# Feed-forward stages: the second down chunk is rounded in quarters ahead of the last tiles' work

## The chip, the cores and the metric

One NeuronCore of a Trainium2 chip runs one program. The metric is the device time of one execution in microseconds; the median of three runs of the kernel before is 2256.84 us (2256.57 to 2262.26). All arithmetic is on float32 data. Engines are called PE (matmul), PEld (PE's weight load), DVE, ACT, POOL and SP (it issues DMAs).

## The reference, cut to what matters

The reference is a chain of two blocks over 256 latent tokens (and 256 context tokens in the first) of width 1024. The first has a latent attention and a short convolution layer, each with a mixture of 32 experts; the second has a state-space mixer, a feed-forward layer, a dilated attention and a second feed-forward layer. The change touches the two feed-forward layers of the second block:

```
u = causal_depthwise_conv(h @ w_up, conv_w)      # 1024 -> 2 x 2816, 3 taps
gate, val = u[..., :2816], u[..., 2816:]
y = (silu(gate) * val) @ w_down                  # 2816 -> 1024
x = x + y
```

A root-mean-square norm stands ahead of it, and another, of the sum, behind it.

## The kernel before, in words

**Three products.** A float32 product runs on PE as three products in the format fp32r. Each operand is split in a high half (a rounded copy) and a low half (what the rounding left): high x high, high x low, low x high, summed in one bank (`product3`, line 574 and on; its matmul is line 584). The high half of a weight chunk is made by ACT (`round_scalar`, its instruction is line 297), the low half by DVE as a subtraction (`rest_vector`, line 303). The same work exists in quarters: `round_piece_scalar` (line 312) and `rest_piece_vector` (line 320) do the columns of piece q of four, and piece 3 marks the whole as ready. `product3` waits for the high half of the weights ahead of its first and second products and for the low half ahead of the third.

**The ring.** Weights arrive by DMAs that SP issues (line 274) into a ring of 6 slots of 128x4096 floats. A chunk takes two slots: the raw data, later overwritten by the low half, and the high half. So three chunks are there at a time, and the fetch of a chunk waits until PE has finished the chunk three before it.

**The feed-forward stage** (class `Ffn`). `w_up` has 11 chunks, each for two tiles of 128 channels of gate and value (22 tiles, m = 0 to 21). `w_down` has 6 chunks: number 0 has 2 of the 22 row tiles of H (128x2048 a slot), numbers 1 to 5 have 4 each (128x4096), in the order 0 and 1, 2 to 5, ..., 18 to 21. PE does the up tiles one after the other, 48 matmuls each, then the down chunks in order; within a chunk it goes over the 8 tiles of the result, each with its own bank, which stays open over all chunks. So the 8 result banks are all taken, and the first down matmul waits until the bank of the last up tile has been copied. Chunk 0 is 48 matmuls, the others 96.

Per up tile m, ACT copies the bank into `PB` (line 2747), DVE does six instructions of taps (lines 2776 and 2779) into `acc`, ACT does the silu (line 2726), POOL multiplies (line 2801) to `H`, ACT makes its high half (line 2728) and POOL its low half (line 2803).

**The order on the engines** is written out by hand. Each engine runs its list in order, and each instruction waits on counters of the others. On ACT, step m of the loop is: on even m the rounding of the next chunk (m = 20 rounds down chunk 0), `make_h(m - 2)` (silu and high half), then the copy of tile m. Behind the loop come `make_h(20)`, `make_h(21)`, the roundings of down chunks 1 to 5, and the first rounding of the next stage (`then.prepare_scalar`). On DVE, step m is: on even m the remainder of that chunk, then the taps of tile m once ACT has copied it; behind the loop the remainders of down chunks 1 to 5 and of the next stage's first chunk, then the eight additions to the residual (line 2788). POOL has the two operations of each tile, in order.

Of the kernel before, what the change touches and what calls it, by code (L numbers as in the profile page):

```python
# [62 lines left out]
KFF = FFN // P  # L63
# [670 lines left out]
class Start:  # L734
# [8 lines left out]
    def scalar(self, e, w):  # L743
        k, a = self.k, self.k.a
        e.dma_start(k.cols[:, :], a["cols"]).then_inc(*k.constants.up())
        e.dma_start(k.mats[:, :, :], a["mats"]).then_inc(*k.constants.up())
        e.dma_start(k.rows[:, :], a["rows"].broadcast_to([P, a["rows"].shape[1]])).then_inc(*k.constants.up("constants"))
        w.wait_ge(*k.constants.at("constants"))
        w.wait_ge(*k.pool.at("cond zero"))
        e.activation(k.silu_cond[:, :, 0:2], k.col("cond"), ACT.Silu).then_inc(*k.act.up("silu cond"))  # L750
# [5 lines left out]
    def vector(self, e, w):  # L756
        w.wait_ge(*self.k.constants.at("constants"))
# [459 lines left out]
class Moe:  # L1217
# [590 lines left out]
    def more_scalar(self, e):  # L1808
        if isinstance(e, Count):
            return  # L1810
        scalar, cap, (rows, turned, x_turned, _) = self.more["scalar"].sem, self.cap, self.more_banks()
        with e.If(self.more_flag(e) > 0):
            self.more_begin(e)
            for n in range(self.n_blocks - 1):
                with e.Fori(0, EXPERTS, 1) as x:
                    it = x + n * EXPERTS
                    e.wait_ge(*self.more_count("matmul", it, 2))
                    e.activation(self.h[0][0:cap, :], rows[cap:2 * cap, :], ACT.Silu).then_inc(scalar, 1)
                    e.wait_ge(*self.more_count("matmul", it, 3))
                    e.activation(k_flat(self.ht[0]), turned[:, 0:KF * cap], ACT.Copy).then_inc(scalar, 1)  # L1820
                    e.wait_ge(*self.more_count("matmul", it, 4))
                    e.activation(self.y[0], x_turned[:, :], ACT.Copy).then_inc(scalar, 1)
                    e.wait_ge(*self.more_count("vector", it, 6))
            for m in range(KD):
                self.squares.square(e, m, self.k.X[:, m, 0:self.T]).then_inc(scalar, 1)
            e.wait_ge(*self.more_count("matmul", (self.n_blocks - 1) * EXPERTS, 1))

    def more_vector(self, e):
        if isinstance(e, Count):
            return  # L1830
        vector, cap, (rows, turned, x_turned, _) = self.more["vector"].sem, self.cap, self.more_banks()
        with e.If(self.more_flag(e) > 0):
            self.more_begin(e)
# [804 lines left out]
class Ffn:  # L2638
# [78 lines left out]
    def scalar(self, e, w):  # L2717
        k, T, key = self.k, SEQ, self.key
        pe, act, dve, pool, banks = k.pe, k.act, k.dve, k.pool, k.banks
        k.meet(w, self.before)  # L2720
        k.norm_parts_scalar(e, w, key, lambda i: k.A[:, i, 0:T], self.x_parts[0])

        def make_h(m):
            s = m % 4
            w.wait_ge(*dve.at(key, "taps", m))
            e.activation(self.acc[:, s, 0, :], self.acc[:, s, 0, :], ACT.Silu).then_inc(*act.up(key, "silu", m))
            w.wait_ge(*pool.at(key, "h", m))
            e.activation(self.H_high[:, m, :].bitcast(F32R), self.H[:, m, :], ACT.Copy).then_inc(*act.up(key, "h high", m))  # L2728

        w.wait_ge(*pool.at(key, "pads"))  # L2730
        for m in range(KFF):
            s = m % 4
            if m % 2 == 0:
                (self.w_up + self.w_down)[m // 2 + 1].round_scalar(e, w)
            if m >= 2:
                make_h(m - 2)
            if m >= 4:
                w.wait_ge(*dve.at(key, "taps", m - 4))
            if m < 2:
                for j in range(2):  # L2740
                    w.wait_ge(*pe.at(key, "up", m, j))
                    e.activation(self.PB[:, s, j, self.pad:], banks.of(key, "up", m, j)[:, 0:T], ACT.Copy
                                 ).then_inc(*act.up(key, "up", m, j))
                act.mark(key, "up", m)
            else:
                w.wait_ge(*pe.at(key, "up", m))
                e.activation(self.PB[:, s, :, self.pad:], banks.of(key, "up", m)[:, :].rearrange("p (j t) -> p j t", j=2),
                             ACT.Copy).then_inc(*act.up(key, "up", m))
        make_h(KFF - 2)
        make_h(KFF - 1)  # L2750
        for chunk in self.w_down[1:]:
            chunk.round_scalar(e, w)
        if self.then:
            self.then.prepare_scalar(e, w)
        for m in range(KD):
            self.squares.square_scalar(e, w, m, k.X[:, m, 0:T], dve.at(key, "out", m))
        k.root_scalar(e, w, ("ffn out", self.layer), T)
        act.mark("end", key)

    def vector(self, e, w):  # L2760
        k, T, key = self.k, SEQ, self.key
        pe, act, dve, pool, banks = k.pe, k.act, k.dve, k.pool, k.banks
        k.meet(w, self.before)
        w.wait_ge(*dve.now())
        k.norm_parts_vector(e, w, key, lambda i: k.A[:, i, 0:T], k.col("ffn_norm")[:, self.layer, :], *self.x_parts)
        taps = k.col("ffn_conv_w")
        for m in range(KFF):
            s = m % 4
            if m % 2 == 0:
                (self.w_up + self.w_down)[m // 2 + 1].rest_vector(e, w)  # L2770
            if m >= 4:
                w.wait_ge(*pool.at(key, "h", m - 4))
            w.wait_ge(*act.at(key, "up", m))
            for j in range(2):
                buf, w3 = self.acc[:, s, j, :], taps[:, self.layer, j * KFF + m, :]
                e.tensor_scalar(buf, self.PB[:, s, j, 0:T], w3[:, 0:1], None, ALU.mult).then_inc(*dve.up())
                for q in (1, 2):
                    w.wait_ge(*dve.now())
                    e.scalar_tensor_tensor(buf, self.PB[:, s, j, q:q + T], w3[:, q:q + 1], buf, ALU.mult, ALU.add  # L2779
                                           ).then_inc(*dve.up())  # L2780
            dve.mark(key, "taps", m)
        for chunk in self.w_down[1:]:
            chunk.rest_vector(e, w)
        if self.then:
            self.then.prepare_vector(e, w)
        for m in range(KD):
            w.wait_ge(*pe.at(key, "out", m))
            e.tensor_tensor(k.X[:, m, 0:T], banks.of(key, "out", m)[:, 0:T], k.X[:, m, 0:T], ALU.add
                            ).then_inc(*dve.up(key, "out", m))
        k.root_vector(e, w, ("ffn out", self.layer), T)  # L2790
        dve.mark("end", key)
# [580 lines left out]
```

## Time and profile before

| | |
|---|---|
| median of the runs | 2256.84 us (2256.57 to 2262.26) |
| the profiled execution | 2263.14 us, its span 2261.3 us |
| busy: PE, DVE, ACT, POOL | 94%, 44%, 32%, 11% of the span |
| mean granted clock of PE | 0.97 |
| matmuls, all of PE | 13462 |

Times of the rows below are counted from the start of the span of the profiled execution. A view can be asked for a stretch of the span. The first feed-forward stage's down chunks lie near 1775 to 1850 us, the second's near 2178 to 2250 us. A granted clock of 1.00 is 2.4 GHz, 0.50 is 1.2 GHz.

### The profile page before, as it was taken

What the parts mean: (1) busy time and instruction counts of PE and PEld (TensorE: products, weight loads), DVE (VectorE), ACT (ScalarE), POOL (GpSimd) and SP (SyncE); (2) the same over time, 40 slices, a digit from 0 to 9 for tenths busy, and PEclk for the clock granted to TensorE, in tenths of its full rate; (3) what the DMA queues carried; (4) which work ended last, traced back from release to release, by engine and by line L of the source; (5) the groups of instructions that cost most, each with busy time, mean ns of one, the idle gap of its engine ahead of it and who ended that gap; (6) DMA issues with size and microseconds to landing.
All of it is one profiled execution on the core that took longest, in us unless ns stands there. A gap on an engine that the chain in (4) does not pass through costs nothing. (4 is left out here: it accounts for less than half of the span.)

```text
span 2261.3 us, 31171 instructions
## 1 busy us (share of the span) xinstructions
PE 2118.1 (94%) x13462; PEld 1487.5 (66%) x13462; DVE 1003.7 (44%) x1647; ACT 717.6 (32%) x1073; POOL 244.4 (11%) x220
## 2 busy tenths in 40 slices
PE   5999999999998898999999988988899889999988
PEld 3745644444443795444444438966899889998987
DVE  3434411111110654111111118866589656777983
ACT  3234211111111542111111128855455444445542
POOL 0000000000000000000000000065136200003630
PEclk9999899999999998999999999999999989999999
DMA  9777699999999567999999984421445444334542
GB/s 326 258 271 261 246 415 421 421 421 421 421 421 383 187 223 297 418 421 421 421 420 421 421 340 166 161 97 53 149 150 187 168 170 127 98 128 158 184 147 94
DMA packets 216208, 616.86 MB, mean 273 GB/s; under 512 B 20224, under 2 KB 107392, under 8 KB 166656
## 3 DMA queue, kind: packets, MB, share of 16 engines
q1 hardware_dynamic: 208960, 612.01, 70.3%
q10 hardware_dynamic: 7104, 2.76, 0.4%
q8 instruction: 110, 1.80, 0.3%
q14 instruction: 34, 0.28, 0.0%
HBM read 613.69 MB, written 1.05 MB: 272 GB/s over the span
## 5 line engine op out<-in xcount | busy, mean ns | idle before, releaser
L1328 PE MATMUL bank<-ring,arena 128*64 128x512 f32 x2048 | 454.4, 593 | 12.2 <-DMA ring<-in_moe_w_up 12.0
L584 PE MATMUL bank<-normed_rounded,ring_rounded 128*128 128x256 f32 x3424 | 416.5, 283 | 4.9 <-ACT normed_rounded L680 3.4
L584 PEld LDWEIGHTS bank<-normed_rounded,ring_rounded 128*128 128x128 f32 x3424 | 412.1, 189 | 6.9 <-issue 4.3
L303 DVE TENSOR_TENSOR ring_rounded<-ring,ring_rounded 128x4096 fp32r<-128x4096 f32 (+2 forms) x68 | 295.3, 4347 | 131.5 <-ACT ring_rounded L297 131.3
L1328 PEld LDWEIGHTS bank<-ring,arena 128*64 128x64 f32 x2048 | 149.4, 137 | 305.6 <-issue 304.7
L1674 DVE TENSOR_TENSOR arena<-arena,bank 64x512 f32<-64x512 f32 x64 | 43.6, 681 | 660.9 <-ACT arena L1498 660.9
L584 PE MATMUL bank<-arena_rounded,ring_rounded 128*128 128x256 f32 x2336 | 296.5, 287 | 19.2 <-DVE ring_rounded L303 6.9
L584 PEld LDWEIGHTS bank<-arena_rounded,ring_rounded 128*128 128x128 f32 x2336 | 288.1, 193 | 22.4 <-DVE ring_rounded L303 7.5
L297 ACT ACTIVATE ring_rounded<-ring 128x4096 fp32r<-128x4096 f32 (+2 forms) x68 | 234.7, 3455 | 58.0 <-DMA ring<-in_ffn_w_down 51.3
L1337 PE MATMUL bank<-ring,arena 128*64 128x512 f32 x1024 | 235.6, 602 | 3.8 <-ACT arena L1505 3.8
L1498 ACT ACTIVATE arena<-bank 64x512 f32<-64x512 f32 x64 | 38.1, 595 | 449.1 <-PE bank L1328 449.1
L1337 PEld LDWEIGHTS bank<-ring,arena 128*64 128x64 f32 x1024 | 68.2, 137 | 123.8 <-issue 110.9
L572 PEld LDWEIGHTS bank<-mats,arena 128*128 128x128 f32 (+2 forms) x662 | 84.6, 166 | 79.2 <-issue 66.3
L1352 PE MATMUL bank<-arena 64*128 64x256 f32 x1024 | 127.8, 388 | 1.4 <-ACT arena L1512 1.4
L1512 ACT ACTIVATE arena<-bank 128x512 f32<-128x512 f32 x64 | 38.3, 598 | 276.8 <-PE bank L1337 276.8
L572 PE MATMUL bank<-mats,arena 128*128 128x128 f32 (+2 forms) x662 | 103.0, 278 | 8.7 <-POOL arena L2414 5.4
L1352 PEld LDWEIGHTS bank<-arena 64*128 64x128 f32 x1024 | 93.2, 186 | 23.8 <-issue 11.7
L2779 DVE SCALAR_TENSOR_TENSOR arena<-arena,cols 128x256 f32<-128x256 f32 x176 | 95.3, 541 | 6.3
L2803 POOL TENSOR_TENSOR arena_rounded<-arena,arena_rounded 128x256 fp32r<-128x256 f32 x44 | 92.8, 2110 | 23.3 <-ACT arena_rounded L2728 23.3
L1307 PE MATMUL bank<-arena_rounded 128*128 128x256 f32 x512 | 78.3, 298 | 0.0
L1307 PEld LDWEIGHTS bank<-arena_rounded 128*128 128x128 f32 x512 | 65.5, 190 | 5.0 <-issue 1.2
L1505 ACT ACTIVATE arena<-bank 128x256 f32<-128x256 f32 x64 | 24.7, 386 | 132.5 <-PE bank L572 132.5
(274 smaller groups left out, 2082.7 us busy)
## 6 DMA issues: line engine op xcount, KB each, us to landing
ring<-in_moe_w_gate SPq DMA_DIRECT2D x128, 1024.0 KB, 16.7
ring<-in_moe_w_up SPq DMA_DIRECT2D x128, 1024.0 KB, 19.0
ring<-in_moe_w_down SPq DMA_DIRECT2D x128, 1024.0 KB, 18.3
ring<-in_w_mod SPq DMA_DIRECT2D x24, 2048.0 KB, 11.5
ring<-in_ffn_w_up SPq DMA_DIRECT2D x44, 1024.0 KB, 7.5
ring<-in_ssm_w_in SPq DMA_DIRECT2D x12, 2048.0 KB, 8.1
ring<-in_ffn_w_down SPq DMA_DIRECT2D x10, 2048.0 KB, 7.8
ring<-in_conv_w_in SPq DMA_DIRECT2D x6, 2048.0 KB, 9.0
```

The lines of the kernel that those rows point to most:

```text
L297: e.activation(ring.rounded[(self.number + 1) % RING][:, 0:n].bitcast(F32R), ring.slots[self.number % RING][:, 0:n], ACT.Copy).then_inc(*s ...
L303: e.tensor_tensor(ring.rounded[slot][:, 0:n].bitcast(F32R), ring.slots[slot][:, 0:n], ring.rounded[(self.number + 1) % RING][:, 0:n], ALU. ...
L572: return e.transpose(out, in_, self.mats[0:rows, 0, 0:rows])
L584: end = e.matmul(out, lhs.bitcast(F32R), rhs.bitcast(F32R), start=start and n == 0 and k == 0, stop=stop and n == 2 and k == n_k - 1)
L1307: end = e.matmul(out, f[:, t, feats].bitcast(F32R), mine[:, t, hot].bitcast(F32R), start=t == 0 and f is self.f_high, stop=t == self.NT - ...
L1328: ends[i] = e.matmul(bank[rows, :], xt[:, n * KD // 2 + j, :], weights[:, j, :], start=n == 0 and j == 0, stop=n == 1 and j == KD // 2 - 1)
L1337: end = e.matmul(bank[n * cap:(n + 1) * cap, :], self.ht[x][:, k, :], weights[:, i, n * 512:(n + 1) * 512], start=k == 0, stop=k == KF - 1)
L1352: end = e.matmul(self.acc(kk), self.y[x][rows, i * P:(i + 1) * P], self.back[x][rows, :], start=False, stop=last and kk % 2 == 1)
L1512: e.activation(self.y[x % 2], banks.of(key, "y", x)[:, :], ACT.Copy).then_inc(*act.up(key, "y", x))
L1674: e.tensor_tensor(h, h, banks.of(key, "h", x)[0:cap, :], ALU.mult).then_inc(*dve.up(key, "h", x))
L2779: e.scalar_tensor_tensor(buf, self.PB[:, s, j, q:q + T], w3[:, q:q + 1], buf, ALU.mult, ALU.add).then_inc(*dve.up())
L2803: e.tensor_tensor(self.H_low[:, m, :].bitcast(F32R), self.H[:, m, :], self.H_high[:, m, :], ALU.subtract).then_inc(*pool.up(key, "h low", m))
```

## The change

In both feed-forward stages the rounding of down chunk 1 is cut in four pieces and moved forward. On ACT, piece 0 goes between the high half of tile 19 and the copy of tile 21, pieces 1 to 3 between that copy and `make_h(20)`. On DVE, the four remainders go between the wait for the copy of tile 21 and the taps of tile 21. The loops behind go over chunks 2 to 5. PE, POOL and SP keep their lists.

```diff
@@ scalar @@
             if m >= 2:
                 make_h(m - 2)
+            if m == KFF - 1:
+                self.w_down[1].round_piece_scalar(e, w, 0)
             if m >= 4:
                 w.wait_ge(*dve.at(key, "taps", m - 4))
...
+        for q in (1, 2, 3):
+            self.w_down[1].round_piece_scalar(e, w, q)
         make_h(KFF - 2)
         make_h(KFF - 1)
-        for chunk in self.w_down[1:]:
+        for chunk in self.w_down[2:]:
             chunk.round_scalar(e, w)
@@ vector @@
             w.wait_ge(*act.at(key, "up", m))
+            if m == KFF - 1:
+                for q in range(4):
+                    self.w_down[1].rest_piece_vector(e, w, q)
             for j in range(2):
...
-        for chunk in self.w_down[1:]:
+        for chunk in self.w_down[2:]:
             chunk.rest_vector(e, w)
```

## Rows read from the trace of the kernel before

**Rows 1.** The page, part 4: shares of the span by engine and line.

```profile
PE bank L584 22%; DVE ring_rounded L303 2%; ACT ring_rounded L297 1%; PE bank L2136 1%; PE bank L2944 1%; PE bank L618 1%; DVE arena L2484 1%; PE bank L619 1%; PE bank L2968 1%; DVE ring_rounded L320 1%; PE bank L2887 1%; PE bank L624 1%; PE bank L572 0%; PE bank L2987 0%; PE bank L2208 0%; PE bank L2158 0%
```

**Rows 2.** Timeline of PE: start us, us, engine, line, operation, count, [idle before, releaser].

```profile
1775.53 5.91 PE L584 MATMUL bank<-arena_rounded,ring_rounded 128*128 128x256 f32 x48 [0.78 <-ACT arena L2747]
1784.40 1.21 PE L584 MATMUL bank<-arena_rounded,ring_rounded 128*128 128x256 f32 x8 [2.97 <-ACT ring_rounded L297]
1788.86 49.15 PE L584 MATMUL bank<-arena_rounded,ring_rounded 128*128 128x256 f32 x400 [3.25 <-DVE ring_rounded L303]
1840.08 10.31 PE L584 MATMUL bank<-arena_rounded,ring_rounded 128*128 128x256 f32 x72 [2.07 <-DVE residual L2788]
...
2191.71 57.63 PE L584 MATMUL bank<-arena_rounded,ring_rounded 128*128 128x256 f32 x472 [3.21 <-DVE ring_rounded L303]
```

**Rows 3.** The chain of waits, 1755 to 1860: start us, us, what.

```profile
1780.84 3.52 ACT ring_rounded L297
...
1823.84 7.74 DMA ring<-in_w_kv
```

**Rows 4.** Timeline of SP, the fetches of down chunks 1, 3, 4, 5; then 3, 4-5.

```profile
1763.39 0.37 SPq L274 DMA_DIRECT2D ring<-in_ffn_w_down  x1
...
1781.47 0.37 SPq L274 DMA_DIRECT2D ring<-in_ffn_w_down  x1
1801.12 0.37 SPq L274 DMA_DIRECT2D ring<-in_ffn_w_down  x1
1812.48 0.37 SPq L274 DMA_DIRECT2D ring<-in_ffn_w_down  x1
...
2184.33 0.37 SPq L274 DMA_DIRECT2D ring<-in_ffn_w_down  x1
2203.94 11.73 SPq L274 DMA_DIRECT2D ring<-in_ffn_w_down  x2
```

**Rows 5.** Windows: stretch us, PE, PEld, DVE, ACT, POOL busy (count), PEclk, DMA, GB/s.

```profile
1788.86:1790.00 1.14, 1.14 (x5) 1.14 (x6) 1.14 (x1) 1.07 (x1) 0.00 (x0) 0.50 0.00 0
...
1812.50:1823.80 11.30, 11.30 (x98) 11.30 (x97) 4.42 (x1) 2.59 (x1) 0.00 (x0) 1.00 0.50 187
...
1840.10:1843.00 2.90, 2.90 (x13) 2.90 (x14) 0.26 (x1) 0.71 (x2) 0.73 (x1) 0.50 0.74 277
```

**Rows 6.** Timeline of ACT at the end of the up tiles.

```profile
1772.31 0.42 ACT L2728 ACTIVATE arena_rounded<-arena 128x256 fp32r<-128x256 f32 x1 [2.32 <-POOL arena L2801]
1774.79 0.60 ACT L2747 ACTIVATE arena<-bank 128x512 f32<-128x512 f32 x1 [2.06 <-PE bank L584]
...
1780.75 7.11 ACT L297 ACTIVATE ring_rounded<-ring 128x4096 fp32r<-128x4096 f32 x2
```

**Rows 7.** Lines 312 and 320 over the whole span: ns min/median/max.

```profile
L312 ACT ACTIVATE ring_rounded<-ring x28: 1038/1046/1072, 41.2 to 1587.1; 128x1024 fp32r<-128x1024 f32 x28
L320 DVE TENSOR_TENSOR ring_rounded<-ring,ring_rounded x28: 1212/1225/2196, 42.3 to 1589.9; 128x1024 fp32r<-128x1024 f32 x28
```

**Rows 8.** Landings: the tile in_ffn_w_down over the span, and the page's part 6.

```profile
DMA to landing us min/median/max: 4.7/7.8/9.0
...
ring<-in_moe_w_up SPq DMA_DIRECT2D x128, 1024.0 KB, 19.0
```

**Rows 9.** Timeline of DVE.

```profile
1757.10 4.97 DVE L303 TENSOR_TENSOR ring_rounded<-ring,ring_rounded 128x4096 fp32r<-128x4096 f32 x1
...
1775.49 0.35 DVE L2776 TENSOR_SCALAR arena<-arena,cols 128x256 f32<-128x256 f32 x1 [0.36 <-ACT arena L2747]
...
1778.10 1.00 DVE L2779 SCALAR_TENSOR_TENSOR arena<-arena,cols 128x256 f32<-128x256 f32 x2
1784.38 13.10 DVE L303 TENSOR_TENSOR ring_rounded<-ring,ring_rounded 128x4096 fp32r<-128x4096 f32 x3 [5.28 <-ACT ring_rounded L297]
```

**Rows 10.** Timeline of POOL.

```profile
1758.32 4.35 POOL L2803 TENSOR_TENSOR arena_rounded<-arena,arena_rounded 128x256 fp32r<-128x256 f32 x1 [0.53 <-ACT arena_rounded L2728]
...
1777.05 0.87 POOL L2803 TENSOR_TENSOR arena_rounded<-arena,arena_rounded 128x256 fp32r<-128x256 f32 x1 [0.53 <-ACT arena_rounded L2728]
```

## The prediction

> **What bounds the kernel now.** I read the page first: its chain that ended last gives line 584, the three-product matmul on PE, 22% of the span, by far the largest line [rows 1]. So time is won only where PE stands idle or runs slowly. The second view is PE's timeline at the end of the first feed-forward stage [rows 2]. There PE does the 48 matmuls of down chunk 0 until 1775.53 + 5.91 = 1781.44, waits 2.97 us for ACT, does 8 matmuls, and waits 3.25 us for DVE; the second stage shows the same (3.21 us before its 472 matmuls). After that comes one long run. The third view, the chain of waits over the same stretch [rows 3], says what ended those waits: ACT's rounding of down chunk 1, then DVE's remainder of it, and nothing else between 1780.84 and 1788.86. It also shows a later link that the change leaves alone: the fetch of the next stage's first chunk, its rounding, and the wait that it causes.
>
> The fourth view is SP's timeline [rows 4]: a down fetch is issued when PE has finished a chunk, so the issues clock the chunks. The fetch at 1781.47 marks the end of chunk 0, that at 1801.12 the end of chunk 1, that at 1812.48 the end of chunk 2. Chunk 1 therefore took 19.65 us, and chunk 2, of the same 96 matmuls, 11.36 us. In the second stage it is 2203.94 - 2184.33 = 19.61 us against (11.73 - 0.37) = 11.36 us. The difference, 8.29 and 8.25 us, is more than the two waits (2.97 + 3.25 = 6.22). The fifth view, the windows with the granted clock [rows 5], shows where the other 2 us are: after the second wait PE is granted 0.50 (1.2 GHz), against 1.00 (2.4 GHz) in chunk 2. The 88 matmuls from 1788.86 to 1801.12 took 12.26 us, where 88/96 of 11.36 is 10.41.
>
> **The change part by part.** Each of the two stages gets the same edits, so I work out the first one.
>
> *Piece 0 on ACT, in front of the copy of up tile 21.* ACT has finished the high half of tile 19 at 1772.31 + 0.42 = 1772.73 and then stood idle 2.06 us until PE released the copy at 1774.79 [rows 6]. A piece of 128x1024 costs 1.046 us on ACT [rows 7]. Chunk 1 was asked for at 1763.39 [rows 4]; a down chunk landed 4.7 to 9.0 us after its issue, median 7.8 [rows 8], so by 1772.4 at the latest. Piece 0 runs 1772.7 to 1773.7, inside the idle time: cost nothing. Without that cover (a late landing) everything behind it waits: the copy, the last taps, and PE, since chunk 0 started only when that copy had emptied its bank. That is a rival below. SP's issues stay where they are, because what they wait for (PE's up tiles and chunk 0) does not move.
>
> *Pieces 1 to 3 on ACT.* Behind the copy, which ends at 1775.39, come 3 x 1.046, each starting some 0.1 before the last ends as ACT's pairs do: 1775.3 to 1778.2. The high half of chunk 1 is complete at 1778.2, 3.2 us before PE asks for it at 1781.44. What is queued behind the pieces is the silu and high half of tile 20, 2.9 us later; only POOL's product of tile 20 and the last down chunk (tiles 18 to 21) wait for that, and PE reached the last chunk near 1835. Cost nothing.
>
> *Four pieces on DVE, in front of the taps of tile 21.* DVE's row is 1.225 us each [rows 7]; in a run of three remainders 13.10 us passed, not 3 x 4.42 = 13.26, so each starts 0.08 early: 4 x 1.225 - 4 x 0.08 = 4.58 us. They start at 1775.49, where the taps started [rows 9], and the low half is complete at 1780.1, 1.4 us before PE finishes chunk 0. Both waits of PE are gone, and with them the idle time ahead of the slow clock. Chunk 1 takes what chunk 2 took: gain 8.29 us.
>
> *What is late next.* The taps of tile 21 took from 1775.49 to 1778.10 + 1.00 = 1779.10, 3.61 us, and now start at 1780.07, so end at 1783.68. From their end to the start of the next rounding on ACT (silu, POOL's product, high half) it was 1780.75 - 1779.10 = 1.65 us [rows 6, 9]. That rounding is now chunk 2's: it starts at 1785.33 and, at half of the 7.11 us that two such take, ends at 1788.9. DVE's remainder, 4.42, ends at 1793.35. PE finishes chunk 1 at 1781.44 + 11.36 = 1792.80, and asks for the low half after 8 of 96 matmuls, at 1793.75. The slack is 0.40 us. Below, the cost can't be under nothing, since PE can't start chunk 2 before chunk 1 is done. Above, POOL's operations can add to it. Before, two of POOL's (one is the 0.87 us of [rows 10]) ran inside those 3.61 us; if one more gets in the way, the remainder is 0.87 late and PE stands 0.47 us. I take 0.1, near the zero end, and keep 0.5 for each stage. Such a wait costs itself only: the 0.78 us wait before chunk 0 was followed by 48 matmuls in 5.91 us.
>
> Chunk 3 is not touched: its fetch at 1781.47 stays, it is rounded on ACT until 1792.6 and its remainder ends at 1793.4 + 4.4 = 1797.8, while PE wants it at 1804.2. Chunks 4 and 5 are fetched when chunks 1 and 2 end, so they move with PE and keep their distance: chunk 4 is issued at 1792.8, and with 9.0 + 3.6 + 4.4 is ready at 1809.8 against 1815.5. The next stage's first chunk (the 7.74 us fetch of [rows 3], its rounding, and the 2.07 us wait of PE with the clock of 0.50 behind it, [rows 2, 5]) hangs on the end of chunk 3 and moves whole. So the gain passes to the next stage undiminished, and the second stage ends in PE work alone.
>
> *The rule of the Trainium skill weighed.* POOL's remainder of a tile at 1758.32 took 4.35 us and ended 0.6 us after DVE's remainder of a chunk (1757.10 + 4.97), where the one at 1777.05, beside the taps, took 0.87 [rows 9, 10]. The Trainium skill ("SBUF — State Buffer", section "SBUF: two separate sides") says that GpSimd and a DVE operation with two SBUF inputs take a shared pair of ports in turn, one blocking the other for its whole instruction. By that rule, which the row bears out, POOL's product of tile 20 stands still while DVE's pieces run, or slips between two of them and delays the rest. The first costs nothing here; the second is the 0.47 us above.
>
> **Sum.** Gain 8.29 + 8.25 = 16.54, less 2 x 0.1: 16.3 us. The profiled execution took 2263.14 us (span 2261.3 and 1.8 around it); it becomes 2246.8. The median of the runs shown is 2256.84, 6.3 us under the profiled one, whose time is close to the highest run, 2262.26. Nothing in these terms depends on that difference, so I take them off the median: 2240.5 us.
>
> **Rivals.**
> - *The clock is not given back.* The waits go, 2 x 6.2 = 12.4 us, but the granted clock falls somewhere else in the now unbroken run: 2244.4. For it: PE's load rises. Against: chunks 2 and 3 ran at 1.00 in an equally dense run. 7%.
> - *Chunk 2's remainder takes the place of chunk 1's.* If the DVE and POOL collisions come to more than I think, PE stands before chunk 2. A wait like the 2.07 us one brought the clock down to 0.50, and the 72 matmuls behind it took 10.31 us instead of 72/96 x 11.36 = 8.5. Some 2.1 + 1.8 = 3.9 us per stage then come off: 16.5 - 7.8 = 8.7 gained, 2248.1. For it: the slack is 0.40 us. Against: it needs 2.5 us of slip, three of POOL's operations. 8%.
> - *Slower: piece 0 waits for its data.* It stands on ACT before the copy that frees PE's last bank. From 1774.79 - 1.05 - 1763.39 = 10.35 us to landing on, each further microsecond delays chunk 0 by as much. It ends above today's time from some 17 us on: with the 19.0 us that the expert chunks took [rows 8], chunk 0 starts 8.65 us late and, after such idle time, 1.8 us slow; chunk 1 ends at 1781.44 + 8.65 + 1.8 + 11.36 = 1803.25, 2.1 us later than today, 4.3 us over both stages: 2261.1. Against: those landings belong to a stretch with many fetches at once, and no down chunk took over 9.0 us. 2%.
> - *The change does nothing that counts*, as the gain is taken back by a transfer in the attention stage: 2256.8. Against: every fetch of the ring is issued on PE's progress and moves with it. 3%.
>
> **How the numbers follow.** The forecast gets 80%. From no wait at all (2240.3) over 0.5 us in each stage (2241.3) it spans little by itself; the runs of before differ by 5.7 us, and a median may sit at either side. I take 2237.5 to 2248.5, which holds the first two rivals. A measurement of this kernel tells about 0.3%, 6.8 us, from no change. Faster by more: the forecast, the clock rival, and the chunk 2 rival (8.7 us), 95%, of which I take 1 off to the middle for its edge: 94%. Within: 4%. Slower: 2%.
>
> **What would show it.** In the profile after, no wait of PE for the rounding or remainder of down chunk 1 in either stage; down issues some 11.4 us apart from the fourth to the sixth; granted clock 1.00 from chunk 0 to chunk 4; ACT's copy of up tile 21 released by PE, not by piece 0; DVE's last taps ending 4.6 us later behind chunk 0's start; the remainder of chunk 2 ending within 0.5 us of PE's need. I am wrong if piece 0 is released by a DMA after the copy was due, if PE waits over 1 us before chunk 2, or if the span shrinks by under 12 us.

## The result, and the profile after

The changed kernel took 2244.76 us in the median of five runs (2242.49 to 2247.20), against 2256.84 (2256.32 to 2262.26) of the kernel before. The ratio on record is 0.9931, with a 95% interval of 0.9918 to 0.9945; the two medians alone give 0.9946, just outside it. Five runs more of it, beside fourteen of the kernel before, gave 0.9918 (0.9906 to 0.9931). The gain is under 1%, but both intervals leave out 1. The forecast, 2240.5 of 2256.84, is 0.9928 and lies in both intervals; its range held the time.

The profiled execution took 2242.49 us. Its PE timeline answers [rows 2]. The first stage's block of 456 matmuls (54.23 us) now runs without a wait up to the last chunk, of which 24 matmuls are done by then, and the second stage has no wait at all (528 matmuls).

```profile
1772.94 54.23 PE L584 MATMUL bank<-arena_rounded,ring_rounded 128*128 128x256 f32 x456 [0.78 <-ACT arena L2749]
1829.28 10.30 PE L584 MATMUL bank<-arena_rounded,ring_rounded 128*128 128x256 f32 x72 [2.11 <-DVE residual L2795]
...
2165.90 62.77 PE L584 MATMUL bank<-arena_rounded,ring_rounded 128*128 128x256 f32 x528 [0.78 <-ACT arena L2749]
```

SP's timeline, as in [rows 4]: the fetches of chunks 3 and 4, then 5, of the first stage. Chunk 1 lasts from 1778.89 to 1778.89 + (11.73 - 0.37) = 1790.25, 11.36 us where it was 19.65, and chunk 2 ends at 1801.65, 11.40 later.

```profile
1778.89 11.73 SPq L274 DMA_DIRECT2D ring<-in_ffn_w_down  x2
1801.65 0.37 SPq L274 DMA_DIRECT2D ring<-in_ffn_w_down  x1
```

The windows of the first stage, columns as in [rows 5], over chunk 1, the first matmuls of chunk 2, and the rest of it. The granted clock is 1.00 throughout.

```profile
1778.80:1790.10 11.30, 11.30 (x98) 11.30 (x97) 5.88 (x7) 7.47 (x4) 1.49 (x2) 1.00 0.54 196
1790.10:1791.20 1.10, 1.10 (x12) 1.10 (x11) 1.10 (x2) 0.52 (x1) 0.00 (x0) 1.00 0.00 0
1791.20:1801.60 10.40, 10.40 (x90) 10.40 (x90) 4.19 (x2) 3.63 (x1) 0.00 (x0) 1.00 0.54 202
```

The timelines of ACT and then of DVE show the moved pieces (lines 312 and 320) and what is queued behind them. They answer [rows 6] and [rows 9].

```profile
1770.05 1.04 ACT L312 ACTIVATE ring_rounded<-ring 128x1024 fp32r<-128x1024 f32 x1
1772.20 0.60 ACT L2749 ACTIVATE arena<-bank 128x512 f32<-128x512 f32 x1 [1.11 <-PE bank L584]
1772.70 2.95 ACT L312 ACTIVATE ring_rounded<-ring 128x1024 fp32r<-128x1024 f32 x3
...
1782.82 3.61 ACT L297 ACTIVATE ring_rounded<-ring 128x4096 fp32r<-128x4096 f32 x1
```

```profile
1772.90 5.18 DVE L320 TENSOR_TENSOR ring_rounded<-ring,ring_rounded 128x1024 fp32r<-128x1024 f32 x4 [0.35 <-ACT arena L2749]
1778.01 0.83 DVE L2783 TENSOR_SCALAR arena<-arena,cols 128x256 f32<-128x256 f32 x1
...
1780.18 1.01 DVE L2786 SCALAR_TENSOR_TENSOR arena<-arena,cols 128x256 f32<-128x256 f32 x2
1786.46 8.76 DVE L303 TENSOR_TENSOR ring_rounded<-ring,ring_rounded 128x4096 fp32r<-128x4096 f32 x2 [5.28 <-ACT ring_rounded L297]
```

POOL's product of tile 20 asked for the same time as DVE's third and fourth piece:

```profile
1776.03 0.98 POOL L2808 TENSOR_TENSOR arena<-arena 128x256 f32<-128x256 f32 x1 [5.06 <-ACT arena L2726]
```

Piece 0 ran inside idle time and left 1.11 us of it; PE still releases the copy. The low half of chunk 2 was ready at 1786.46 + 4.42 = 1790.88 (17.94 us after the first down matmul). Counted from SP's fetch, as the prediction does it, PE wanted it at 1790.25 + 0.95 = 1791.20, 0.3 us later. That overstates the slack: the experiment with all four of ACT's pieces behind the copy puts it under 0.1 us.

**Where the 20.65 us between the two profiled executions went.** I cut each span at four marks: PE's first down matmul of either stage (before: 1775.53 and 2178.39; after: 1772.94 and 2165.90) and the first matmul of the norm behind it (1850.76 and 2249.71; 1839.94 and 2229.01). The first stage's stretch went from 75.23 to 67.00, 8.2 us less, the second's from 71.32 to 63.11, 8.2 less. The other 4.3 us lie in unchanged code: 2.6 before the first mark (where piece 0 is the only thing changed) and 1.7 in the attention stage.

### The profile page after: what moved, and what is told of

Read it like the earlier page. It is cut to its first block and busy times, and to the rows that moved or that the text cites. A ratio compares the mean times of both kernels' runs of the same rounds, so it can differ in the third digit from the quotient of the medians.

```text
span 2240.7 us, 31183 instructions
## 1 busy us (share of the span) xinstructions
PE 2109.5 (94%) x13462; PEld 1481.8 (66%) x13462; DVE 1003.7 (45%) x1653; ACT 718.4 (32%) x1079; POOL 244.7 (11%) x220
## 5 line engine op out<-in xcount | busy, mean ns | idle before, releaser
L303 DVE TENSOR_TENSOR ring_rounded<-ring,ring_rounded 128x4096 fp32r<-128x4096 f32 (+2 forms) x66 | 286.6, 4345 | 115.2 <-ACT ring_rounded L297 115.0
L584 PE MATMUL bank<-arena_rounded,ring_rounded 128*128 128x256 f32 x2336 | 290.9, 284 | 6.8 <-ACT arena_rounded L1927 2.6
L584 PEld LDWEIGHTS bank<-arena_rounded,ring_rounded 128*128 128x128 f32 x2336 | 283.3, 190 | 9.2 <-ACT arena_rounded L1927 3.4
L297 ACT ACTIVATE ring_rounded<-ring 128x4096 fp32r<-128x4096 f32 (+2 forms) x66 | 227.7, 3450 | 39.4 <-DMA ring<-in_ffn_w_down 32.8
```

Source lines behind the costliest of these rows:

```text
L297: e.activation(ring.rounded[(self.number + 1) % RING][:, 0:n].bitcast(F32R), ring.slots[self.number % RING][:, 0:n], ACT.Copy).then_inc(*s ...
L303: e.tensor_tensor(ring.rounded[slot][:, 0:n].bitcast(F32R), ring.slots[slot][:, 0:n], ring.rounded[(self.number + 1) % RING][:, 0:n], ALU. ...
L584: end = e.matmul(out, lhs.bitcast(F32R), rhs.bitcast(F32R), start=start and n == 0 and k == 0, stop=stop and n == 2 and k == n_k - 1)
```

## The experiments

All of them are read by the same marks. "Stage" is the stretch from the first down matmul to the norm's matmul of the second stage, 71.3 us before and 63.1 after.

**The changed kernel again.** No edit. 

> The changed kernel once more. Theory (the whole change is the two waits and the slow clock of down chunk 1, 8.2 us in each feed-forward stage, and the rest of what single runs show is scatter of stages that the change does not touch): PE's down matmuls again run as one block of 456 in the first stage and 528 in the second, with 62.77 us for the 528 as in the first profile of it; from PE's first down matmul to the final norm's matmul 63.1 us in the second stage against 71.3 before. Median near 2244, where the middle of nine or ten runs of each kernel differs by 12 to 17 us. Rival (something of the gain is given back in a stage behind): the stretch from the first stage's end to the second's begin is longer by 2 to 4 us than the 338.3 us of before.

Measured: a median of 2241.36 us against 2261.05, ratio 0.9918. The stages took 67.14 and 63.11, the attention stretch 325.86, against 327.63 before and 325.96 in the first profile of the change. (The 338.3 of the expectation was counted from another mark, PE's last chunk of the first stage; there it is 338.31 before and 336.51 here.) Nothing was given back behind the first stage: the rival falls.

**One stage at a time.** The edits of the change under `if self.layer == 0`, or 1:

```diff
-            if m == KFF - 1:
+            if m == KFF - 1 and self.layer == 0:
                 self.w_down[1].round_piece_scalar(e, w, 0)
...
-        for chunk in self.w_down[2:]:
+        for chunk in self.w_down[2 if self.layer == 0 else 1:]:
```

> The change in the first feed-forward stage alone. Theory: the first stage is 8.2 us shorter and all behind it as before; the second stage keeps its waits of 3.0 and 3.2 us and 19.6 us for down chunk 1. Time: half of the whole change's gain, 6 to 8 us under before. Rival (the gain is given back in the attention stage behind it): under 4 us.

> The change in the second feed-forward stage alone. Nothing but the final norm stands behind it, so nothing can give the gain back: 8.2 us under before in the stage. Theory: its gain and that of the other stage alone are equal and add to that of the whole. Rival: this one gains 8, the other less.

The first stage alone: ratio 0.9960 (0.9946 to 0.9974), stretches of 67.34 and 71.09. The second alone: 0.9966 (0.9953 to 0.9979), 75.25 and 63.10. Each is worth about the half, and 0.40% + 0.34% = 0.74% stands beside the 0.82% of the whole change, timed next to the same runs of before. In the trace of the first, the untouched stage keeps both waits. Its 8 matmuls between them took 1.66 us instead of the 1.21 of [rows 2], at a granted clock of 0.50 from 2175.50 to 2176.50, so the clock had already fallen before the second wait:

```profile
2174.93 1.66 PE L584 MATMUL bank<-arena_rounded,ring_rounded 128*128 128x256 f32 x8 [2.96 <-ACT ring_rounded L297]
2179.39 57.41 PE L584 MATMUL bank<-arena_rounded,ring_rounded 128*128 128x256 f32 x472 [2.80 <-DVE ring_rounded L303]
```

**DVE's remainders behind the last taps.** This keeps ACT's part of the change and takes DVE's back.

```diff
@@ vector @@
-            if m == KFF - 1:
-                for q in range(4):
-                    self.w_down[1].rest_piece_vector(e, w, q)
...
+        for q in range(4):
+            self.w_down[1].rest_piece_vector(e, w, q)
         for chunk in self.w_down[2:]:
```

> ACT's four pieces stay moved forward; DVE's four remainders of down chunk 1 go back behind the taps of tile 21, in front of chunk 2's remainder. Theory, in times from the first down matmul: the taps end at 3.6, the remainders at 3.6 + 4.6 = 8.2, and PE wants the low half at 5.7 + 0.95 + 0.2 = 6.9: a wait of 1.3 us at the ninth matmul of chunk 1, too short to bring the granted clock down, nothing before chunk 2. 6.9 us gained in each stage, 2.6 us less than the whole change. Rival (any idle time of PE here brings the clock down): 2 us more lost in each stage, that is 6.6 less than the whole change.

Ratio 0.9945 (0.9932 to 0.9959), stage 66.88, 3.8 us more than with the whole change. The wait was 2.03 us where I had said 1.3, as DVE's four remainders took 6.26 us and not 4.6, and the clock fell, as the rival had it:

```profile
1776.19 6.26 DVE L320 TENSOR_TENSOR ring_rounded<-ring,ring_rounded 128x1024 fp32r<-128x1024 f32 x4
```

PE's timeline and its windows behind the wait:

```profile
1773.61 6.86 PE L584 MATMUL bank<-arena_rounded,ring_rounded 128*128 128x256 f32 x56 [0.78 <-ACT arena L2749]
1782.51 49.12 PE L584 MATMUL bank<-arena_rounded,ring_rounded 128*128 128x256 f32 x400 [2.03 <-DVE ring_rounded L320]
```

```profile
1782.50:1784.00 1.50, 1.50 (x11) 1.50 (x12) 0.00 (x0) 1.50 (x1) 0.55 (x1) 0.86 1.01 407
1784.00:1785.00 1.00, 1.00 (x6) 1.00 (x6) 0.00 (x0) 1.00 (x1) 0.00 (x0) 0.50 1.02 406
```

So ACT's part is worth 4.4 of the 8.2 us, and DVE's part the other 3.8: the wait, 0.2 for the break in the block, and 1.5 of clock (in the second stage the 472 matmuls took 57.64 us, where 62.77 less 56 matmuls' 6.6 is 56.1).

**All four of ACT's pieces behind the copy.**

```diff
@@ scalar @@
-            if m == KFF - 1:
-                self.w_down[1].round_piece_scalar(e, w, 0)
...
-        for q in (1, 2, 3):
+        for q in range(4):
```

> All four of ACT's pieces behind the copy of up tile 21, none ahead of it. Times from the first down matmul, going by the trace of the changed kernel (chunk 1 ends at 17.3, chunk 2's low half is ready at 17.9 and wanted at 18.2, slack 0.3): DVE's first piece starts 0.85 us later, so the low half of chunk 1 is ready at 6.3 against 6.9 (no wait), and that of chunk 2 at 18.8: PE waits 0.5 us before the low product of chunk 2, the granted clock stays at 1.00. The second stage takes 0.5 us more than the 63.1 of the changed kernel. Rival (piece 0 ahead of the copy is worth its full 1.05 us, or nothing): 1.0 or 0.0 us more.

Ratio 0.9928 (0.9911 to 0.9944); stage 64.09, 1.0 us more. The wait is where the theory has it, ahead of the low products of chunk 2, but 0.74 instead of 0.5:

```profile
1771.48 18.23 PE L584 MATMUL bank<-arena_rounded,ring_rounded 128*128 128x256 f32 x152 [0.78 <-ACT arena L2747]
1790.44 36.24 PE L584 MATMUL bank<-arena_rounded,ring_rounded 128*128 128x256 f32 x304 [0.74 <-DVE ring_rounded L303]
```

DVE's first piece came 0.97 us later than in the changed kernel (0.93 after the first down matmul, against 0.04 before it), not 0.85, and the second stage grew by 0.98 us, all of it. So piece 0's place is worth its full 1 us, as the rival had it, and the slack before chunk 2 was next to nothing instead of 0.3 us. Two rows show where the 0.3 came from: the matmuls of these blocks in the changed kernel (ns min/median/max), and DVE's remainders of chunks 2 and 3 in this one.

```profile
L584 PE MATMUL bank<-arena_rounded,ring_rounded x87: 277/280/285, 1779.8 to 1789.9; 128*128 128x256 f32 x87
```

```profile
1785.96 8.76 DVE L303 TENSOR_TENSOR ring_rounded<-ring,ring_rounded 128x4096 fp32r<-128x4096 f32 x2 [5.28 <-ACT ring_rounded L297]
```

A matmul is shown 0.28 us long, but the next one starts 0.12 us behind its start (96 in 11.36 us). SP's fetch comes when the last matmul of a chunk has ended, and by then PE has been in the next chunk for some 0.2 us. Without a wait the 153rd matmul would have started 18.23 - 0.28 + 0.12 = 18.07 us after the first. It starts 0.06 us after DVE's remainder has ended here (1790.44 against 1785.96 + 4.42), and in the changed kernel that remainder ended at 17.94: a slack of under 0.1 us. For the same reason a break in a block costs some 0.2 us beside the wait that the row shows.

**Chunk 1 whole.**

```diff
@@ scalar @@
+        self.w_down[1].round_scalar(e, w)      # in place of the four pieces, behind the copy
         make_h(KFF - 2)
@@ vector @@
             if m == KFF - 1:
-                for q in range(4):
-                    self.w_down[1].rest_piece_vector(e, w, q)
+                self.w_down[1].rest_vector(e, w)
```

> Down chunk 1 rounded whole at the same places: ACT behind the copy of tile 21, DVE in front of the taps. Theory (quarters matter because DVE can start a quarter into ACT's work, and each engine's list has little slack): the low half is ready at 7.8 to 8.4 after the first down matmul against 6.9 wanted, a wait of 0.9 to 1.5; the taps end later, chunk 2's low half is ready near 21.4 and wanted at 19.5, a wait of 2.0, which brings the granted clock down for another 1.8 us: second stage 5.0 us longer than the changed kernel's 63.1. Rival (splitting buys nothing, moving forward is all): 0 to 1 us longer.

Ratio 0.9944 (0.9927 to 0.9961), stage 66.24, 3.1 us more than the changed kernel, against a forecast of 5.0. There were two waits, 1.12 and 1.53, and the clock did not fall: the theory's places were right, the second wait 0.5 shorter, its 1.8 us of clock wrong. This kernel also has nothing ahead of the copy; beside the kernel with all four pieces behind it (64.09) the whole chunk costs 2.1 us, and that is what the quarters save.

```profile
1781.95 11.62 PE L584 MATMUL bank<-arena_rounded,ring_rounded 128*128 128x256 f32 x96 [1.12 <-DVE ring_rounded L303]
1795.11 36.23 PE L584 MATMUL bank<-arena_rounded,ring_rounded 128*128 128x256 f32 x304 [1.53 <-DVE ring_rounded L303]
```

**DVE slipped, by 8 and by 16 instructions.**

```diff
                 e.tensor_scalar(buf, self.PB[:, s, j, 0:T], w3[:, 0:1], None, ALU.mult).then_inc(*dve.up())
+                for _ in range(8 if m == KFF - 1 and j == 0 else 0):
+                    w.wait_ge(*dve.now())
+                    e.tensor_scalar(buf, self.PB[:, s, j, 0:T], w3[:, 0:1], None, ALU.mult).then_inc(*dve.up())
```

> The changed kernel with one instruction of the taps of tile 21 (0.35 us, the same values again) repeated eight times on DVE. Theory (slack of 0.3 us before chunk 2, and a wait of 2 us or more costs 1.8 us of slow clock beside itself): the low half of chunk 2 is 3.0 to 3.6 us later, PE waits 2.7 to 3.3 us there and runs at a granted clock of 0.50 behind it, 4.5 to 5.1 us per stage. Rival (the granted clock falls only where the waits come in pairs, as before): 2.7 to 3.3 us per stage.

> As b_slip, with 16 repeated instructions instead of 8. b_slip's wait of 2.89 us before the low products of chunk 2 left the granted clock at 1.00, while 2.03 us after the eighth matmul of chunk 1 was followed by 0.50. Theory (length counts once it is long enough, as the 4.05 us of c_late_fetch was): a wait of 6.0 us, a granted clock of 0.50 behind it, and the 304 matmuls take 37.6 to 38.2 us instead of 36.23. Rival (the place decides, after a long unbroken run a wait costs only itself): 36.2 us.

With 8, the extra row is 3.08 us long, the wait 2.89 and the stage 66.21, 3.1 more: the whole slip, with no slack to take off. The ratio is 0.9966 (0.9953 to 0.9978). Behind that wait of 2.89 us the granted clock is 1.00 in every window, and the 304 matmuls take their 36.23 us. The rival's price held. Its reason, that only paired waits bring the clock down, did not: a single wait of 2.03 us did so in the kernel with DVE's remainders behind the taps. The extra row, then PE:

```profile
1780.36 3.08 DVE L2786 TENSOR_SCALAR arena<-arena,cols 128x256 f32<-128x256 f32 x8
```

```profile
1795.54 36.23 PE L584 MATMUL bank<-arena_rounded,ring_rounded 128*128 128x256 f32 x304 [2.89 <-DVE ring_rounded L303]
...
2191.67 44.76 PE L584 MATMUL bank<-arena_rounded,ring_rounded 128*128 128x256 f32 x376 [2.89 <-DVE ring_rounded L303]
```

With 16, PE waited twice, 2.49 for ACT's half of chunk 2 and 3.25 for DVE's, as it did before the change for chunk 1; I had overlooked ACT. The clock fell to 0.50 and the 304 matmuls took 38.38 us, 2.2 more than at full clock; in the second stage the 376 took 47.46, 2.7 more than the 44.76 above. The stage was 72.02, and the only run, 2262.11 us, is close to the kernel before (2261.58): the slip has put the old pair of waits one chunk later.

```profile
1794.83 1.21 PE L584 MATMUL bank<-arena_rounded,ring_rounded 128*128 128x256 f32 x8 [2.49 <-ACT ring_rounded L297]
1799.29 38.38 PE L584 MATMUL bank<-arena_rounded,ring_rounded 128*128 128x256 f32 x304 [3.25 <-DVE ring_rounded L303]
1839.91 8.78 PE L584 MATMUL bank<-arena_rounded,ring_rounded 128*128 128x256 f32 x72 [2.24 <-DVE residual L2798]
```

In its second stage the clock fell behind the first wait alone, 2.48 us after 17.27 us of matmuls: the 8 matmuls behind it took 1.86 us, and the granted clock in them was 0.50.

```profile
2196.39 1.86 PE L584 MATMUL bank<-arena_rounded,ring_rounded 128*128 128x256 f32 x8 [2.48 <-ACT ring_rounded L297]
2200.85 47.46 PE L584 MATMUL bank<-arena_rounded,ring_rounded 128*128 128x256 f32 x376 [2.60 <-DVE ring_rounded L303]
```

```profile
2196.80:2198.20 1.40, 1.40 (x7) 1.15 (x6) 1.40 (x1) 1.40 (x1) 0.00 (x0) 0.50 1.00 401
```

**The fetch of chunk 1 late**, with piece 0 ahead of the copy and, in a second kernel, with all four behind it as above.

```diff
         for chunk in self.w_up + self.w_down:
+            if chunk is self.w_down[1]:
+                w.wait_ge(*self.k.pe.at(self.key, "up", KFF - 2))
             chunk.fetch(e, w)
```

> The changed kernel, but SP issues the fetch of down chunk 1 when PE has finished up tile 20 instead of 19, 5.7 us later. This tries the rival on the other side: piece 0 stands ahead of the copy and waits for its data. Theory: with 7.8 us to landing the data is there 2.1 us after the copy was due, piece 0 ends 3.1 us after it, the copy and the first down matmul are 3.1 us late, and after 3.9 us of idle time the granted clock falls: 3.1 + 1.8 = 4.9 us per stage against the changed kernel, some 10 in all; still some 6 us under before. Rival (the landing takes under 5.7 us, as the 4.7 of a small chunk): nothing.

> As c_late_fetch, but with all four of ACT's pieces behind the copy of up tile 21. Theory (what makes a late landing dear is that piece 0 stands ahead of the copy): the first down matmul is on time with a wait of 0.78 us instead of 4.05; DVE's pieces end 7.0 to 7.7 us after it against 6.9 wanted, a wait of 0 to 0.8 in chunk 1, and chunk 2's low half is 2.3 us later than in the changed kernel, which makes a wait of 1.5 to 2.0: 2 to 2.8 us per stage instead of 4.8, if the clock stays. Rival (the late data cost the same wherever they are waited for): 4.8 us.

With piece 0 ahead, ratio 0.9945 (0.9929 to 0.9962): the first down matmul comes after 4.05 and 3.84 us instead of 0.78, and the granted clock falls behind it (stage 64.60, 1.5 more). Together 4.8 and 4.6 us in each stage, as forecast. The ratio is only 0.0027 or 0.0014 above that of the changed kernel (0.9918 and 0.9931), less than the 9.4 us (0.41%) of the stages in the traces. The scatter of the code ahead of the stages, some 6 us over the traces, is large enough for that, but it is not shown to be the reason. ACT's timeline shows why the first down matmul is late: the data came 4.39 us after ACT was free. Below it, the window behind the wait:

```profile
1774.23 1.06 ACT L312 ACTIVATE ring_rounded<-ring 128x1024 fp32r<-128x1024 f32 x1 [4.39 <-DMA ring<-in_ffn_w_down]
1775.19 0.58 ACT L2751 ACTIVATE arena<-bank 128x512 f32<-128x512 f32 x1
```

```profile
1775.90:1778.00 2.10, 2.09 (x10) 2.10 (x11) 2.10 (x2) 2.10 (x3) 0.00 (x0) 0.50 1.02 417
```

With all four behind the copy, ratio 0.9953 (0.9937 to 0.9970): the wait at the start is 0.78 again, and the second stage has waits of 0.84 and 1.17 at full clock, 65.59, 2.5 us more, about half the cost. So the place of piece 0 makes a late landing dear, as the rival on the other side had it. At the landings of this kernel, which leave 1.11 us, it costs nothing. The runs don't tell the two kernels apart; the traces do.

**The next wait: DVE's first addition ahead of the next stage's remainder.**

```diff
@@ vector @@
-        if self.then:
-            self.then.prepare_vector(e, w)
         for m in range(KD):
+            if m == 1 and self.then:
+                self.then.prepare_vector(e, w)
             w.wait_ge(*pe.at(key, "out", m))
```

> The changed kernel, and in the first feed-forward stage DVE adds result tile 0 to the residual ahead of the remainder of the next stage's first chunk (before: behind it). That takes away the 2.1 us wait of PE for its bank in the last down chunk. Theory: the wait of 2.1 and the slow clock behind it (72 matmuls in 10.30 us, 8.5 at full clock, 1.8) go; DVE has the other additions in arrears until 4 us before the stage's end and catches up: 3.9 us less than the changed kernel in the first stage, the second as it is. Median 3 to 4 us under that of the changed kernel. Rival (the remainder, now 1 us later, or the additions in arrears hold up the norm or the first matmuls of the attention stage): under 2 us.

2237.58 us (2235.10 to 2240.34) against 2261.58, ratio 0.9896 (0.9878 to 0.9914), the fastest kernel of all. The wait of 2.11 us is gone, the first stage is one block of 528 matmuls, and its stretch is 64.09 against 67.00 and 67.14: 3.0 us, not 3.9. The rest was lost at the norm, whose matmul waits 1.34 us for POOL (0.36 before): with the additions in arrears, POOL has five of the sums for the norm to do in one go. The rival named this hold-up, but it left more than 2 us. The interval lies below the one of the changed kernel, 0.9918 to 0.9945, and overlaps the other, 0.9906 to 0.9931. The two kernels were not timed beside each other, so the 3 us are the traces' reading.

```profile
1772.30 62.75 PE L584 MATMUL bank<-arena_rounded,ring_rounded 128*128 128x256 f32 x528 [0.78 <-ACT arena L2749]
1836.39 0.70 PE L495 MATMUL bank<-arena,mats 128*128 128x256 f32 x2 [1.34 <-POOL arena L487]
```

```profile
1832.11 4.24 POOL L487 TENSOR_TENSOR arena<-arena,rstd 128x256 f32<-128x256 f32 x5 [0.59 <-ACT rstd L479]
```

## Why the prediction was right, point by point

- *The gain is 8.29 and 8.25 us, two waits and the slow clock behind them.* Right: the stretches are 8.2 and 8.2 us shorter in the first profile, and the one-stage kernels show each by itself. Reading the chunk's length off SP's fetches, rather than adding PE's waits (6.22), found the 2 us beside them. They are not all clock, though: the experiments put such a stretch of slow clock at 1.5 us (62.77 against 64.24 us for 528 matmuls, 8.78 against 10.30 for 72), and each of the two breaks in the block at 0.2. So a wait that goes is worth 0.2 us more than its row shows.
- *Piece 0 costs nothing.* Right, 1.11 us of its cover left. The late fetch shows what it would cost without.
- *Pieces 1 to 3.* 2.95 us, as worked out.
- *Four pieces on DVE, 4.58 us.* Mis-sized: 5.18, as POOL's product of tile 20 fell among them. It slipped in between two pieces, as the prediction had weighed. The taps behind took 1780.18 + 1.01 - 1778.01 = 3.18 instead of 3.61, since the product no longer fell among the taps. The sum of the two, 8.29 against 8.19, was right, partly by luck: the two errors cancel.
- *Slack of 0.40 us before chunk 2, cost 0.1 us.* Mis-sized: worked out as 0.40 us (0.44 by its own unrounded terms), the slack was under 0.1 us; the cost was nothing. The step that failed is taking the end of chunk 1 from SP's fetch, which comes some 0.2 us after PE has gone on. Two runs show it: 0.97 us later on DVE made the stage 0.98 longer, and 3.08 us made it 3.10. That no wait came at all is luck, though the forecast had room for a short one.
- *A second wait of about 2 us would bring the clock down.* Not borne out as a rule, see the last section: before chunk 2 the slip of 3 us cost 3.1 and no clock, where this rival had 1.8 of clock beside the wait.
- *The next stage's first chunk moves whole.* Right: the wait is 2.11 for 2.07, and the block behind it 10.30 us for 10.31.
- *The sum, 16.3 us.* The stretches of the two stages give 16.4 us in the first profile. The medians gave 12.1 us the first time (15.6 if the ratio of 0.9931 is applied to 2256.84) and 19.7 the second (18.5 by the ratio). The forecast lies between them, but neither pair of medians shows it; the traces do. So that the median of 2244.76 us came within 4.3 us of the forecast is in part luck. The profiled execution, forecast at 2246.8 us, took 2242.49. The rest most likely lies in code that the change doesn't touch: over twelve traces (that with piece 0 waiting for a late fetch left out) the first down matmul falls between 1770.21 and 1776.01 us, with the same code ahead of it but for piece 0, which runs in idle time.

## What to carry to other kernels

Time a repeated block by the events that its end triggers (here the fetches), not by the sum of waits: the difference is what the clock and the breaks took. But such an event can lag the engine by some tenths of a microsecond, so it doesn't measure a slack of that size. When work is moved forward in a list, follow the chain from the work that it pushes back to the next deadline; here 8 us of gain stood on less than 0.1 us of slack, which a delay put in for the purpose measures. Ask of an instruction put ahead of one that frees a bank whether its own data can be late.

## What the runs showed of the hardware that I had not expected

**How long a wait is does not decide by itself whether the granted clock falls.** In the order of length, one trace of each kernel:

- 0.78 us: never. 1.12 then 1.53 us, 11.62 us apart: no.
- 2.03 us after 6.86 us of matmuls: yes, in both stages.
- 2.07 to 2.44 us in the last chunk of the first stage: yes in ten kernels, no in two. The two had waits of 2.24 and 2.28 us, and their 72 matmuls took 8.78 us. The kernel with DVE's remainders behind the taps had a wait of 2.28 us too, and its 72 took 10.31. The run ahead doesn't decide either: it was 36.23 and 38.38 us of matmuls in the two, and 36.23 in others where the clock fell.
- 2.48 us after 17.27 us (second stage, 16 instructions): yes. 2.89 us after 18.22 us (8 instructions): no, in both stages.
- 3.84 and 4.05 us after the long run of up tiles: yes.
- Two waits of 2.5 to 3.3 us with 8 matmuls between: yes, each time.

A stretch of slow clock mostly cost 1.5 us, but 2.2 and at least 2.7 us behind the pair of waits in the kernel with 16 instructions. What decides stays open.

**The attention stage has two lengths.** From the norm's matmul to the next stage's first down matmul, seven kernels have 325.57 to 325.96 us and five have 327.59 to 328.99 (the kernel with the late fetch is left out, as its wait falls in there). Among the five are the kernel before and the one with all four of ACT's pieces behind the copy, which differs from the changed kernel in the place of piece 0 alone. In its first 20 us PE is busy as long, at a different granted clock, and near its end the clock differs as well. Here are both stretches in the kernel before and then in the changed one:

```profile
1850.76:1870.76 20.00, 16.60 (x93) 15.07 (x94) 16.99 (x35) 11.09 (x20) 0.00 (x0) 0.74 0.46 164
2043.76:2055.76 12.00, 7.87 (x35) 7.07 (x36) 7.79 (x18) 7.32 (x11) 2.50 (x2) 0.57 0.53 175
```

```profile
1839.94:1859.94 20.00, 16.59 (x100) 15.07 (x101) 16.99 (x35) 11.09 (x20) 0.00 (x0) 0.83 0.47 164
2032.94:2044.94 12.00, 8.60 (x49) 8.17 (x50) 9.15 (x18) 7.01 (x10) 1.82 (x1) 0.72 0.50 165
```

At a clock of 0.50 these means are some 10 us of slow clock at either end before, and some 7 us after; the twelve traces divide the same way, the long ones with 10 and the short ones with 7. Whether 1.7 us of the profiled difference belong to the change is not shown. The three kernels with the first stage as in the change are all short, the two with it as before both long, and the kernels that alter it otherwise stand in both groups. Why the clock differs was not tried.
